# Down stage of a hybrid block: the low part of every second weight chunk from an accumulating DMA

## The reference

```python
hf = rmsnorm(x, norm_ffn[l])
act = silu(hf @ w_gate[l]) * (hf @ w_up[l])
x = x + act @ w_down[l]          # (256, 5632) @ (5632, 2048): the Down stage
return rmsnorm(x, norm_final)
```

## Time and profile before

| | |
|---|---|
| time, median of 3 runs | 1759.29 us (1758.98 to 1760.27) |
| span of the profiled execution | 1757.6 us |
| own time of the profiled execution | not given; the runs lie 1.4 to 2.7 us above the span |
| TensorE busy | 1745.9 us, 99% |
| VectorE busy | 862.1 us, 49% |
| ScalarE busy | 747.8 us, 43% |
| GpSimd busy | 33.2 us, 2% |
| DMA | 331.11 MB, mean 188 GB/s |

### The profile page before, as it was taken

One profiled execution on the slowest core, in us unless ns is written; L12 is line 12 of the kernel. 1 busy time (PEld: TensorE's weight loads), 2 busy tenths in 40 slices (PEclk: granted clock), 3 DMA queues, 4 the chain that ended last, 5 costly groups with the idle time before them and its releaser, 6 DMA issues.

```text
span 1757.6 us, 20453 instructions
## 1 busy us (share of the span) xinstructions
PE 1745.9 (99%) x7883; PEld 1448.9 (82%) x7883; DVE 862.1 (49%) x652; ACT 747.8 (43%) x655; POOL 33.2 (2%) x43
## 2 busy tenths in 40 slices
PE   9999999999999999999999999999999999999997
PEld 8888888888888888888888888888888888888886
DVE  5454455556565444444445554444444444444445
ACT  6444444445454433333333443433333333444444
POOL 1000010100000000000000000000000000000000
PEclk9999999999999999999999999999999999999999
DMA  8656655556555655655556565555555555555552
GB/s 284 195 172 191 190 165 172 167 168 184 164 177 191 198 195 187 195 187 194 187 197 228 190 217 190 187 187 187 186 188 181 191 185 189 207 191 191 191 192 94
DMA packets 150699, 331.11 MB, mean 188 GB/s; under 512 B 7328, under 2 KB 7424, under 8 KB 144640
## 3 DMA queue, kind: packets, MB, share of 16 engines
q1 hardware_dynamic: 150656, 330.50, 57.1%
HBM read 328.38 MB, written 2.10 MB: 188 GB/s over the span
## 4 chain that ended last, share of the span: by engine, by line
PE 99%; ACT 0%; DVE 0%; DMA 0%; POOL 0%; SPq 0%; issue 0%; DVEq 0%; POOLq 0%
PE ps L1132 27%; PE ps L1133 27%; PE ps L1141 27%; PE ps L1408 4%; PE ps L1401 4%; PE ps L1403 4%; PE ps L1150 2%; ACT sq_y L738 0%; PE ps L1230 0%; PE ps L1222 0%; PE ps L1240 0%; PE ps L1247 0%; PE ps L1246 0%; PE ps L1239 0%; DMA vec_rows<-in_conv_w 0%; PE ps L1232 0%
## 5 line engine op out<-in xcount | busy, mean ns | idle before, releaser
L755 DVE TENSOR_TENSOR w_lo<-w_raw,w_hi 128x2048 fp32r<-128x2048 f32 x308 | 707.3, 2299 | 653.4 <-ACT w_hi L424 651.2
L424 ACT ACTIVATE w_hi<-w_raw 128x2048 fp32r<-128x2048 f32 (+1 forms) x309 | 589.7, 1912 | 515.2 <-PE ps L1133 366.5
L1132 PE MATMUL ps<-w_hi,xT_hi 128*128 128x512 f32 x1024 | 404.5, 395 | 0.0
L1133 PE MATMUL ps<-w_hi,xT_lo 128*128 128x512 f32 x1024 | 398.7, 389 | 0.0
L1132 PE MATMUL ps<-w_hi,fT_hi 128*128 128x512 f32 x704 | 274.9, 391 | 0.0
L1133 PE MATMUL ps<-w_hi,fT_lo 128*128 128x512 f32 x704 | 274.0, 389 | 0.0
L1141 PE MATMUL ps<-w_lo,xT_hi 128*128 128x512 f32 x1024 | 253.0, 389 | 0.0
L1132 PEld LDWEIGHTS ps<-w_hi,xT_hi 128*128 128x128 f32 x1024 | 192.3, 188 | 39.9 <-issue 0.2
L1141 PEld LDWEIGHTS ps<-w_lo,xT_hi 128*128 128x128 f32 x1024 | 192.2, 188 | 39.9
L1133 PEld LDWEIGHTS ps<-w_hi,xT_lo 128*128 128x128 f32 x1024 | 192.3, 188 | 39.0
L1141 PE MATMUL ps<-w_lo,fT_hi 128*128 128x512 f32 x704 | 173.9, 389 | 0.0
(11 more groups left out here) (179 smaller groups left out, 1039.1 us busy)
## 6 DMA issues: line engine op xcount, KB each, us to landing
w_raw<-in_w_in SPq DMA_DIRECT2D x127, 1024.0 KB, 5.5
w_raw<-in_w_gate SPq DMA_DIRECT2D x44, 1024.0 KB, 5.2
w_raw<-in_w_up SPq DMA_DIRECT2D x44, 1024.0 KB, 5.2
w_raw<-in_w_down SPq DMA_DIRECT2D x44, 1024.0 KB, 4.8
w_raw<-in_w_branch_a SPq DMA_DIRECT2D x16, 1024.0 KB, 5.1
w_raw<-in_w_branch_b SPq DMA_DIRECT2D x16, 1024.0 KB, 5.0
w_raw<-in_w_out SPq DMA_DIRECT2D x16, 1024.0 KB, 5.1
xn<-in_x SPq DMA_DIRECT2D x4, 512.0 KB, 8.4
```

Source lines behind the costliest of these rows:

```text
L424: copy = lambda o, i, **kw: nc.scalar.activation(o, i, ACT.Copy, **kw)
L755: V.tensor_tensor(w_lo[:, chunk.split, :], w_raw[:, chunk.raw, :], w_hi[:, chunk.split, :].bitcast(F32), ALU.subtract).then_inc(lo_split, 1)
L1132: T.matmul(ps[:, banks + r, :], rows(hi, k, r), w, start=(q == 0 and k == 0), stop=False)
L1133: last = T.matmul(ps[:, banks + r, :], rows(lo, k, r), w, start=False, stop=False)
```

## The change

For chunks 3, 5, 7, ..., 43 of the Down stage (21 of the 44) the low part is made in another way. ScalarE writes the negated rounded weights into a new tile `w_sum` (two places, in memory that the feed-forward activations have left). GpSimd then issues a DMA that reads the same 1 MiB of w_down from HBM a second time and adds it to `w_sum`, which leaves weight minus rounded weight. TensorE waits for that DMA (`summed`) instead of `lo_split` and multiplies with `w_sum`. VectorE no longer subtracts for these chunks; it only counts `lo_split` up when both the rounding and the negation of the chunk are done, so that the raw place comes free. `w_lo` serves the even chunks (and chunk 1).

```diff
+        SUM_SLOTS = 2
+        w_sum = at("w_sum", [P, SUM_SLOTS, CH // 4], F32R, R3)
...
+        SUM_FIRST = 3
+        by_sum = lambda n, i: n % 2 == 1 and not (starts(i) and n < SUM_FIRST)
...
+            for c in range(SUM_FIRST, FC, 2):
+                pool.wait_ge(neg_done, (c - SUM_FIRST) // 2 + 1)
+                nc.gpsimd.dma_start(out=w_sum[:, c // 2 % SUM_SLOTS, :], in_=w_down_k[:, c, :],
+                                    accum_op=ALU.add).then_inc(summed[c // 2 % SUM_SLOTS], 16)
...
+            def negate(n, i):
+
+                c = Chunk(G_DOWN + n + 2, i, RAW_SLOTS)
+                act.wait_ge(raw_landed[c.raw], c.landed())
+                act.wait_ge(lo_used, G_DOWN if starts(i) else c.count(1 - 2 * SUM_SLOTS))
+                copy(w_sum[:, (n + 2) // 2 % SUM_SLOTS, :], w_raw[:, c.raw, :], scale=-1.0).then_inc(neg_done, 1)
...
+                    if n % 2 == 1 and not (last and n == RAW_SLOTS - 1):
+                        negate(n, i)
...
-                    if last and n == RAW_SLOTS - 2:
+                    if by_sum(n + 1, i):
                         stage(c.next())
-                        split(c.next())
+                        dve.wait_ge(hi_split, c.count(2))
+                        dve.wait_ge(neg_done, i * 2 + (1 if n == 2 else 0))
+                        dve.wait_ge(lo_split, c.count(1))
+                        dve.sem_inc(lo_split, 1)
                     elif not (last and n == RAW_SLOTS - 1):
                         split(c.next())
...
-            def down_parts(chunk):
-
+            def down_parts(chunk, n=0):
+
+                low_part, own = (w_sum, n // 2) if by_sum(n, chunk.turn) else (w_lo, chunk.split)
                 h, l = a_hi[:, chunk.split, :], a_lo[:, chunk.split, :]
                 tile = lambda part, r: part[:, r * P:(r + 1) * P]
-                cols_of = lambda w, n: w[:, chunk.split, n * COLS:(n + 1) * COLS]
+                cols_of = lambda w, n: w[:, own if w is low_part else chunk.split, n * COLS:(n + 1) * COLS]
 
                 def high(r, ns, start=False):
...
+            def low_ready(chunk, n):
+                if by_sum(n, chunk.turn):
+                    pe.wait_ge(summed[n // 2], chunk.turn * 16 + (16 if n == RAW_SLOTS - 1 else 0))
+                else:
+                    pe.wait_ge(lo_split, chunk.count(1))
+
+            def down(chunk, n):
+                high, low = down_parts(chunk, n)
                 pe.wait_ge(hi_split, chunk.count(1))
                 pe.wait_ge(a_lo_staged, chunk.count(1 - G_DOWN))
                 high(0, ALL)
                 high(1, ALL).then_inc(hi_used, 1)
-                pe.wait_ge(lo_split, chunk.count(1))
+                low_ready(chunk, n)
                 low(0, ALL)
                 low(1, ALL).then_inc(lo_used, 1)
 
```

More of the change, by code:

```diff
@@ L267, in hybrid_block @@
         a_hi_staged, a_lo_staged = sem("a_hi_staged"), sem("a_lo_staged")
+        neg_done, summed = sem("neg_done"), [sem(f"summed{n}") for n in range(SUM_SLOTS)]
         down_done, y_sum, y_squared, y_total = sem("down_done"), sem("y_sum"), sem("y_squared"), sem("y_total")
@@ L1407, in low @@
                     for n in ns:
-                        ins = T.matmul(ps[:, 4 * r + n, :], tile(h, r), cols_of(w_lo, n), start=False, stop=stop)
+                        ins = T.matmul(ps[:, 4 * r + n, :], tile(h, r), cols_of(low_part, n), start=False, stop=stop)
                     return ins
@@ L1413, in _ @@
             ALL = range(NB)
-            def down(chunk):
-                high, low = down_parts(chunk)
+            def low_ready(chunk, n):
[5 more added lines that the diff above has]
+                high, low = down_parts(chunk, n)
                 pe.wait_ge(hi_split, chunk.count(1))
@@ L1440, in _ @@
             for n in range(1, RAW_SLOTS):
-                down(Chunk(G_DOWN + n))
+                down(Chunk(G_DOWN + n), n)
             with pe.Fori(1, FC // RAW_SLOTS - 1) as i:
                 for n in range(RAW_SLOTS):
-                    down(Chunk(G_DOWN + n, i, RAW_SLOTS))
+                    down(Chunk(G_DOWN + n, i, RAW_SLOTS), n)
             last_turn = [Chunk(G_DOWN + n, FC // RAW_SLOTS - 1, RAW_SLOTS) for n in range(RAW_SLOTS)]
-            for chunk in last_turn[:-2]:
-                down(chunk)
+            for n, chunk in enumerate(last_turn[:-2]):
+                down(chunk, n)
             for r in range(RT):
-                for chunk in last_turn[-2:]:
-                    high, low = down_parts(chunk)
+                for own, chunk in enumerate(last_turn[-2:], RAW_SLOTS - 2):
+                    high, low = down_parts(chunk, own)
                     if r == 0:
@@ L1457, in _ @@
                         if r == 0:
-                            pe.wait_ge(lo_split, chunk.count(1))
+                            low_ready(chunk, own)
                         low(r, ALL)
```

## The result

The changed kernel takes 1782.99 us (1781.48 to 1784.74) against 1759.13 us: 23.9 us more, a ratio of 1.0135 (1.0122 to 1.0147). The direction and the range held; the forecast of +7 us was too small by a factor of three. The profiled execution has a span of 1782.9 us, 25.3 more than before.

The account below looks back on a forecast made before the run. PE was taken as the bound (busy 1745.9 of 1757.6 us). Terms 0 (ScalarE), 0 (VectorE), -0.3, +1.9 (last sum) and +7 (loop) gave +8.6, shaded to +7: 1766 us, range 1759 to 1792.

Parts of the forecast that it names:

- the forecast's own 1763 to 1777: Main case for the whole kernel: sums take two passes and land a little late; 1763 to 1777 us, chance 0.40.
- the upper bound of its sum, +17: Upper bound of all terms added, some +17 us, around a sum of +8.6 with lower bound -0.3.
- the saturated rival: Down stage: the accumulate takes three passes and overfills the DMA engines; 1824 us (1777 to 1850), chance 0.23.
- ScalarE 0: Down stage: 21 added negations of 1.92 us fit in ScalarE's idle time, 1.2 us left; cost 0.
- VectorE 0: Down stage: 21 subtractions removed, 48 us of VectorE work, all beside PE; gain 0.
- Two passes for a sum: Each accumulating DMA takes twice a plain load's engine time, 5.8 us; bounds 2.9 and 8.7.
- Capacity: DMA engines per 10.88 us chunk pair: two passes 0.8 us over at mean cost; at fullest rate 10.1 us, fitting.
- The last chunk: Stage end: the last sum, wanted 5.75 us after its negation, lands in 7.6; PE waits 1.9 us.
- The old wait of 0.3: Last chunk: PE's wait for VectorE's last low part, 0.2 to 0.3 us, goes away; -0.3 us.
- The waits in the loop: PE waits for late sums in the Down stage: 0.4 us times 19 sums, 7 us; bounds 0 to 15.
- 11.9: Budget in us from a sum's issue, at the negation's end, to PE's need two chunks later.
- The 0.4 us of the Trainium skill: GpSimd-issued DMAs: 0.4 us more at each landing, some 4 us on top, an estimate inside the bounds.

Follow-up runs that it names:

- e1: Changed kernel without the 21 accumulating DMAs, PE waiting for the negation instead (another output): 1759.8 us, ratio 0.9998 to before.
- e10: e3 plus, after each sum, a second accumulating DMA of the same bytes onto memory nobody reads: 1836.45 us, ratio 1.0435 to before.
- e2: Changed kernel with GpSimd's DMA copying the weights without the add (another output): 1759.56 us, ratio 0.9999 to before.
- e3: Changed kernel with the negation, and with it the DMA, one chunk (5.44 us) earlier: 1759.5 us, ratio 0.9998 to before.
- e6: Changed kernel with sums only for every fourth chunk (11 instead of 21): 1775.66 us, ratio 1.0092 to before.
- e8: e2 with negation and plain copy one chunk later, so less time from issue to need (another output): 1790.12 us, ratio 1.0171 to before.
- e9: e6 with the negation ahead of the staging of a_hi, so the DMA is issued 0.42 us earlier: 1767.46 us, ratio 1.0041 to before.
- e11b: Changed kernel, all 21 sums, with the negation ahead of the staging of a_hi (DMA 0.42 us earlier): 1773.87 us, ratio 1.0081 to before.
- e7: Changed kernel with the DMA adding actT from the core's own memory instead of HBM weights (another output): 1788.49 us, ratio 1.0161 to before.

## Why the prediction was off by a factor of three

The path was right: what costs is PE's wait for a sum that lands too late. The size of that wait was wrong, and the clock behind some of these waits was not foreseen. That the time still lies in the stated range is luck: 1783 is above the forecast's own 1763 to 1777 and above the upper bound of its sum, +17 (1776; with the two upper bounds that the working itself gives, 15 in the loop and 4.5 at the end, it would have been +19.5, which is still too little). It falls in the part of the range that was given to the saturated rival, and that rival is not what happened.

- **ScalarE 0, VectorE 0, no gain from the freed engine**: right (e1), also in detail: ScalarE idles 1.30 us before the rounding that follows a negation, 1.2 was foreseen.
- **Two passes for a sum**: right. e10 gives 4.9 to 5.0 us, two passes at the rate of the fullest slice, not the 5.8 at the mean cost of a load. Alone the last sum's packets did take 5.8 us, twice the 2.9 of the lone load. The rule of the Trainium skill ("Collectives: The Full Stack", Part 3, why ReduceScatter is half of AllGather), that the second read is what costs, agrees with e2 against the changed kernel: 5.0 us alone without the add, 8.0 with it, and the last copy's packets took 3.1 us where the last sum's took 5.8. No run here has the second read without the adding, so the two are not told apart.
- **Capacity**: the saturated rival is out (a sum takes two passes, not three). The pair's 9.9 us fit in 10.88, as the better of the two capacity counts had it; e3 runs at PE's pace with all 21 sums.
- **The last chunk**: +1.9 foreseen, 2.4 measured (landing 8.0 instead of 7.6). The old wait of 0.3 went, as foreseen.
- **The waits in the loop: the mis-sized term.** I took 0.4 us a sum, 7 us, the middle between nothing and the upper bound of 0.8 us. Measured are 19.5 us over 20 sums, 1.0 each (1.0 a sum is over that bound). The form held: a late sum is followed by one in time, so the mean is about half of the lateness. The sizes did not. The budget is 11.4 us, not 11.9 (issue at 1588.32, wait from 1599.74 on): GpSimd issues 0.3 us after the negation ends (1598.91 to 1599.20), and it is the weight load that waits, 0.2 us ahead of its matmul. The 11.6 of the expectations above was a little high too. The stage's first sum has only 10.1 us, because ScalarE comes to its negation 1.9 us into the chunk instead of 0.6; that was not foreseen, and makes the first wait 1.3 us longer. And landing, where PE waits, is not between 11.9 and 13.5 but 12.1 to 14.9 us. I had counted the engines' time beside a sum at most as two loads of 2.9; e6 shows that two loads do bring 12.4, and what the full kernel has above that comes with sums that follow each other closely and loads that they have held up (landing 9.5 us in the middle, 13.7 at most). Which of the two makes it is not shown.
- **Not priced: the clock.** Three waits of over 2 us were followed by a slower stretch, 4.8 us in all, a fifth of the loss.
- **The 0.4 us of the Trainium skill** more to the first byte for GpSimd's DMAs ("DMA: Bandwidth & Descriptors", the specifications): the trace agrees, 5.0 against 4.7 us alone; in e8 the least is 5.1. It is also about what the last sum was short by: its packets took the 5.8 us foreseen, and 2.2 us lay outside of them instead of 1.8.

No version beats the kernel before. e3 is the change without its loss, and equal to before, since PE was the bound and stays it.

## What to carry to other kernels

Compare the landing of a new DMA under load, not alone, with the time from its issue to its need, and when there is an empty moment one stage earlier, issue there: 5.4 us of lead took away all of a 24 us loss that no engine's busy share could show. Work taken from an engine that nobody waits for gives nothing back, while the wait put in its place can cost, and on TensorE a wait may cost more than its own length, through the clock. A short shift of an issue past another queue's can move landing by more than the shift (e9: 0.42 us earlier, 0.9 us less landing), but did not where the sums followed each other closely (e11b).

## What the runs showed of the hardware

An accumulating DMA of 1 MiB from HBM onto SBUF lands alone in 8.0 us, a plain copy by GpSimd in 5.0, a load by SP in 4.7; GpSimd is busy 0.87 us with the first and 0.54 with the second. Its packets take 5.8 us of the engines alone, against 3.1 for the plain copy. The packets' share of the engines reached 0.99 in e3 with room left, so only a run that is bound by the engines (e10, 14.87 us for six passes) gave their rate. The granted clock fell to a mean of 0.76 over the 7 us behind waits of 2.23, 2.40 and 3.48 us, but not behind ones of 2.69 and 2.94; in other runs it fell behind 2.70 (e9) and 3.00 us (e11b) and not behind 3.02 (e6) and 3.41 (e7).
